# VectorE takes gathered rows between the gates of the fourth last and the third last expert tile

## What is computed

```python
h = layer_norm(ALPHA * x + merged @ w_out, ln1_g, ln1_b)
# peer(h): for each token, 8 heads x 16 experts
u = peer_u[experts]
act = gelu(einsum('thkd,td->thk', u, xb))
v = peer_v[experts]
ff = einsum('thk,thkd->td', g * act, v)      # g: softmax of the top 16 scores
y = layer_norm(ALPHA * h + ff, ln2_g, ln2_b)
```

## Time and profile before

| | us |
|---|---|
| median of 3 runs | 3308.46 (3300.31 to 3311.59) |
| profiled execution | 3307.86 |
| its span | 3306.1 |
| PE busy | 2939.1 (89%) |
| DVE busy | 2367.7 (72%) |
| POOL busy | 1536.1 (46%) |
| ACT busy | 1212.8 (37%) |
| DMA, mean over the span | 331 GB/s, 1092.68 MB |

### The profile page before, as it was taken

How to read it: one execution, slowest core, us unless ns; L and a number is a source line. 1 busy time by engine, 2 the same in 40 slices (tenths; PEclk the granted TensorE clock), 3 DMA queues, 4 the chain that set the end, 5 groups by cost and what they waited for, 6 DMA issues and landing times. The chain is left out here.

```text
span 3306.1 us, 35267 instructions
## 1 busy us (share of the span) xinstructions
PE 2939.1 (89%) x10203; PEld 1637.5 (50%) x10203; DVE 2367.7 (72%) x4737; ACT 1212.8 (37%) x2951; POOL 1536.1 (46%) x1109
## 2 busy tenths in 40 slices
PE   8988989776798898777688899999999999999995
PEld 5754655443445555444444545554444444554552
DVE  0021487696777977977768868778878778878887
ACT  0142233484733444884653332222222222322223
POOL 0000065675763578887888733333333323333331
PEclk9988999897798999998799999999999999999998
DMA  4566689879899999668689999999999999999996
GB/s 143 188 241 238 215 305 347 317 247 292 263 359 386 383 336 357 182 201 224 177 285 302 397 394 415 415 415 415 415 415 415 415 415 412 402 415 398 415 413 250
DMA packets 379985, 1092.68 MB, mean 331 GB/s; under 512 B 91440, under 2 KB 217616, under 8 KB 293648
## 3 DMA queue, kind: packets, MB, share of 16 engines
q0 software_dynamic: 160800, 738.59, 59.0%
q1 hardware_dynamic: 176416, 302.67, 25.9%
q10 hardware_dynamic: 42576, 49.17, 4.3%
HBM read 1027.51 MB, written 61.71 MB: 329 GB/s over the span
## 5 line engine op out<-in xcount | busy, mean ns | idle before, releaser
L472 POOL DMA_INDIRECT expert_rows<-in_experts,picked_index x545 | 660.4, 1212 | 872.1 <-DVE ff_sum L624 757.6
L612 DVE SCALAR_TENSOR_TENSOR expert_rows<-expert_rows,h_tile 128x1024 f32<-128x1024 f32 x577 | 703.6, 1220 | 180.3 <-DMA expert_rows<-in_experts,picked_index 157.2
L492 POOL DMA_INDIRECT gates_by_expert<-dense_gate,gate_address x384 | 693.1, 1805 | 212.1 <-issue 113.2
L624 DVE SCALAR_TENSOR_TENSOR ff_sum<-expert_rows,coefficients,ff_sum 128x1024 f32<-128x1024 f32 x577 | 739.3, 1281 | 31.6 <-ACT coefficients L574 31.0
L1879 PE MATMUL dense_out_ps<-dense_value_rows,dense_weights 128*128 128x512 f32 x1536 | 684.3, 595 | 18.7 <-DMA dense_value_rows<-in_experts 13.4
L1890 PE MATMUL dense_act_ps<-dense_hT,key_columns 128*128 128x384 f32 x2048 | 688.2, 490 | 13.3 <-DMA key_columns<-in_key_columns 9.6
L1890 PEld LDWEIGHTS dense_act_ps<-dense_hT,key_columns 128*128 128x128 f32 x2048 | 386.3, 191 | 327.1 <-DMA key_columns<-in_key_columns 51.7
L1879 PEld LDWEIGHTS dense_out_ps<-dense_value_rows,dense_weights 128*128 128x128 f32 x1536 | 291.9, 191 | 366.2 <-issue 325.3
L897 PE MATMUL proj_ps<-xT,w_in_block 128*128 128x384 f32 (+1 forms) x1392 | 420.5, 465 | 27.7 <-PEq L1671 12.6
L568 ACT ACTIVATE activated<-dots 128x1 f32<-128x1 f32 (+1 forms) x629 | 125.7, 200 | 713.0 <-DVE expert_rows L612 546.2
L897 PEld LDWEIGHTS proj_ps<-xT,w_in_block 128*128 128x128 f32 x1392 | 267.0, 192 | 180.5 <-issue 31.9
(11 more groups left out here) (207 smaller groups left out, 3018.1 us busy)
## 6 DMA issues: line engine op xcount, KB each, us to landing
key_columns<-in_key_columns SPq DMA_DIRECT2D x128, 512.0 KB, 36.9
dense_value_rows<-in_experts SPq DMA_DIRECT2D x128, 512.0 KB, 36.1
gates_by_expert<-zeros POOLq DMA_DIRECT2D x12, 2048.0 KB, 22.4
wq_half<-in_peer_wq SPq DMA_DIRECT2D x48, 512.0 KB, 12.6
dense_gates<-gates_by_expert SPq DMA_DIRECT2D x128, 192.0 KB, 36.1
w_in_block<-in_w_in ACTq DMA_DIRECT2D x18, 1024.0 KB, 12.8
w_in_block<-in_w_in SPq DMA_DIRECT2D x18, 1024.0 KB, 8.1
w_out<-in_w_out SPq DMA_DIRECT2D x24, 512.0 KB, 7.0
```

Source lines behind the costliest of these rows:

```text
L472: pool.indirect_dma_start(to, None, self.a["experts"], bass.IndirectOffsetOnAxis(ap=index[:, k:k + 1], axis=0)).then_inc(got, 16)
L492: pool.indirect_dma_start(self.a["gates_by_expert"], bass.IndirectOffsetOnAxis(ap=self.flat[i][:, k:k + 1], axis=0), self.dgate[i][:, k:k ...
L612: dve.scalar_tensor_tensor(place, place, 1.0, self.h[n % 2][:], ALU.mult, ALU.mult, accum_out=self.dots[:, s % TOPK:s % TOPK + 1]).then_in ...
L624: dve.scalar_tensor_tensor(total, self.slots[self.slot_of[p]][:, D:2 * D], self.coef[:, y % TOPK:y % TOPK + 1], total, ALU.mult, ALU.add). ...
```

## The change

Before expert tile 125's gates (e == ET - 3) VectorE runs the list up to `beside_gates`, and ACT, before it waits for all gates, runs it up to `ahead_of_gates`. Nothing is added to or taken out of the work: the same list is run, with other ends.

```diff
@@ -1818,6 +1818,8 @@
         empty = bg.LAG + bg.NORM_AFTER + 3
         rows_left = lambda n: 1 - (empty + n) / len(bg.events)
         part = lambda it: (min(it, ET - 2) + 1 + max(0, min(it, ET - 2) + 1 - LAG)) / (2 * ET + 3)
+        beside_gates = part(ET - 2) + 5 / len(bg.events)
+        ahead_of_gates = part(ET - 2) + 2 / len(bg.events)
         beside_norm = [rows_left(n) for n in (7, 3, -bg.LAG - 2)]
         ahead_of_norm = [rows_left(n) for n in (10, 6, 0)]
 
@@ -1935,6 +1937,8 @@
                 if it == ET - 3:
                     nc.scalar.mul(eye[:], m["ident"][:], ALPHA).then_inc(eye_set, 1)
                 bg.act(part(it))
+            bg.act(ahead_of_gates)
+            bg.act(ahead_of_gates)
             act.wait_ge(gated, ET)
             for k in range(DENSE):
                 bg.act(ahead_of_norm[k])
@@ -1955,6 +1959,8 @@
 
             for it in range(ET - 1):
                 for e in range(weighed(it - 1), weighed(it)):
+                    if e == ET - 3:
+                        bg.dve(beside_gates)
                     dve.wait_ge(gelud, e + 1)
                     dve.wait_ge(gts_in[held(e)], 16 * (e // GB + 1) if e < ET - 2 else 16)
                     nc.vector.tensor_tensor(w[e % AB][:], w[e % AB][:], gts[held(e)][:], ALU.mult).then_inc(gated, 1)
```

## The result

| | before | changed |
|---|---|---|
| median, us (7 runs each) | 3303.73 (3298.50 to 3311.59) | 3317.83 (3315.81 to 3321.77) |
| ratio | | 1.0046 (1.0036 to 1.0056) |
| profiled execution: span, us | 3306.1 | 3318.3 |
| DVE busy | 2367.7 | 2360.7 |
| PE busy | 2939.1 | 2944.9 |

The change is slower, by 14 us in the medians; 3320 was predicted. The same work is done on each engine; only the idle time lies elsewhere. Lines of the changed kernel are numbered 2 to 6 higher in this part: 1960 is now 1966, 1879 is 1881, 1909 is 1911, 1951 and 1954 are 1955 and 1958.

A forecast was written before the change was run, and what follows sets the result against it. Transfer landings, through one DMA part far behind, were taken to set the pace: gates held until row 667 lands, token tile 0 summed 13.7 us later, the end 12 us later, 3307.86 + 12 = 3319.9; predicted 3320, range 3308.5 to 3325.

The forecast's parts named there:

- Ten rows, not five: Between the gates of tiles 124 and 125 VectorE takes ten rows, steps 658 to 667, 2.34 us each.
- rival (b): Between the gates VectorE runs only five rows, done at 3250.3, so the time is 3308; chance 0.02.
- Landing paces them, and an earlier issue doesn't help: VectorE's ten rows wait for gathers landing 3.8 us apart; row 666, issued at 3238.5, still lands at 3263.1 to 3263.9.
- Rival (a): Gathers come when asked for: VectorE ends the ten rows at 3258.9, plus 0.8 us, 3308.7; chance 0.25.
- no change: Whole kernel: measured time within 0.3% (9.9 us) of before; chance 0.35.
- The row of pairs: One gather and one SP load land together, 3.8 us apart: row 666 with y_tile 0, row 667 with y_tile 1 at 3267.7.
- TensorE's restart: Behind the gates TensorE goes on at 3270.8 and needs 9.2 us to sum token tile 0, at 3280.0.
- From there on: Behind tile 0's sum: 10.3 us for tile 1, 5.9 to its norm, 22.0 to the end at 3318.2.
- The price against the median: Whole kernel: the change costs 12 us, giving 3319.9, or 3320.5 from the median.
- No gain to be had: VectorE's end: ten rows gain almost nothing at any landing, since the rows behind norm(1) stay.
- Rival (c): Earlier gathers slow the late DMA part, pairs at 4.7 us, not 3.8: plus 16 us, 3324; chance 0.06.

The follow-up runs named there:

- light gathers: Changed kernel, ten rows between the gates, but gathers of rows 661 to 671 an eighth as wide; ratio to the kernel before 1.0020.
- five rows: Changed kernel with VectorE's inserted call ending at entry 622, not 627: five rows between the gates of tiles 124 and 125; ratio to the kernel before 1.0008.
- ten rows with moved ends: Changed kernel, ten rows between the gates, with later list ends before the norms behind the loop; ratio to the kernel before 1.0016, median 3308.7 us.
- ScalarE's part alone: Changed kernel with VectorE's inserted call taken out and ScalarE's two calls kept; ratio to the kernel before 1.0006.
- seven rows: Changed kernel with VectorE's inserted call ending at entry 624, not 627: seven rows between the gates; ratio to the kernel before 1.0016.
- five rows and moved ends: Changed kernel with five rows between the gates and list ends before the norms moved to 626 and 630; ratio to the kernel before 0.9992, median 3299.7 us.

## Why the prediction was right

**Ten rows, not five.** The profile has ten rows between the bursts; rival (b) falls.

**Landing paces them, and an earlier issue doesn't help.** Confirmed by row 666 (24.8 us to landing in place of 11.5) and by the light gathers. Rival (a), gathers in time, falls as what happens, but the light gathers came close to it, and it cost 6.6 us (3.6 to 9.6), not the 0.8 that I gave it. The step at fault: I compared its TensorE start only with the late y_tile of the first profile. There tile 0 was summed 29.8 us after the issue of the first y_tile; in the second profile of the kernel before 27.6 us (3232.06 to 3259.7, its row's 1.96 us included); with light gathers 34.0 us (3232.30 to 3266.3), against 32.2 in (a), and rows 659 and 660, late by 1.7 us, make up that difference. So the point from which the ten rows cost something lay earlier than (a) said, and the chance that I put on "no change" was partly placed on a case that was slower.

**The row of pairs.** I let row 667 land at 3267.7, beside the second y_tile. It was there by 3267.3, though the loop ended 1.5 us later in this execution (first y_tile issued at 3237.96, not 3236.48). But the pairs were others. The first y_tile landed at 3256.2 (18.2 us), beside row 664 and not beside row 666, and the second at 3260.9, beside row 665; "y_tiles landing at 3264 to 3271 as before" was wrong. Rows 663 to 666 kept the forecast pace all the same, and row 667 came 2.3 us behind row 666, not 3.8: eight pieces of 0.31 us, the pace of gathers with no load between them. That the last row's landing fits to 0.5 us is in part luck. Counted from the first y_tile's issue the gates came 2.1 us earlier than forecast (3269.64 - 3237.96 = 31.7 against 3270.2 - 3236.48 = 33.7, give or take rounding).

**TensorE's restart.** 9.2 us forecast for token tile 0, 9.9 measured (3270.24 to 3280.16); the extra is the clock, at 1.2 GHz until about 3276, 5.7 us after the restart, which stood in the range and not in the sum.

**From there on** every term held: 10.3 us for tile 1 (3290.5), 5.9 and 5.8 us from a sum to the end of its norm (3286.0 and 3296.3), 22.0 us from there to the end. The span of 3318.3 against 3318.2 forecast is closer than the terms are: the later loop end (plus 1.5), the earlier gates (minus 2.1) and the slower restart (plus 0.7) cancel.

**The price against the median.** 12 us were forecast, 14 measured, with 12 at the edge of the interval (1.0036). The profile before that carried the sum was among the slower executions of its kernel: 3307.86 us, against a median of 3303.73 in the result and 3302 over 29 later runs. So 3320 lies 2 us from the measured 3317.83 because a start 4 us too high and a cost 2 us too low cancel in part.

**No gain to be had.** "The rows behind norm(1) stay" fits five rows that bring nothing, and the ten rows with moved ends show what it is worth: with the ends moved along, two thirds of the cost of ten rows go away.

**Rival (c)**, SP's loads slowed by the earlier gathers, falls: the first y_tile landed 18.2, 27.9, 24.0 and 19.2 us after its issue with ten, eight, seven and five rows, against 27.3 and 25.5 us before and 27.0 with ScalarE's part alone. The Trainium skill's guess (DMA: Bandwidth & Descriptors, section Latency and other measured facts) that the descriptor rings of POOL's transfers slow two of the DMA engines is neither shown nor refuted by that: the traces show one increment of sixteen far behind the rest, but not which engine it came from, nor why.

## What to carry to other kernels

Idle time on an engine ahead of a wait can be filled only with work whose inputs have landed: ask for each moved item when its transfer lands, not when it is issued, and what the engine's next instruction releases. Where the queues are backed up, as here, an earlier issue need not bring an earlier landing (12 us earlier moved nothing). And filling idle time shortens a kernel only if the items leave the stretch that ends last.

## What the runs showed of the hardware

A gather that needs 11.5 us when issued into a lull needs 24.8 us when issued 12 us earlier: both land when the engine that is behind has worked off both queues. In the first profile it is 19.4 us behind the others with y_tile 0, and it takes turns, 8 KB of a gather and 4 KB of a load. While SP's loads were outstanding gathers mostly landed 3.8 us apart, without them 2.3 to 2.5; with gathers of an eighth of the size y_tile 0 landed 14.2 us after its issue, the fastest of all profiles. I had not expected the backlog of SP's queue to differ so much between executions, from 18 us to over 27 us at the same point of the program, nor one landing in the series to come 4.7 us after its neighbour: before y_tile 0 in the first profile, at row 665 in the changed kernel's, at row 664 with five rows and moved ends. What that one is, the runs don't tell.

TensorE's restart did not cost more after a longer pause. Twelve matmuls of 128x512 took 5.31 us in the loop; behind the gates they took 7.97 us after 10.59 us of idle time (five rows), 6.95 after 19.13 (seven rows), 7.41 after 20.57 (light gathers) and 8.20 after 28.94 (ten rows).
